# Tails of the output projections by column halves, row sums of the conditioning vector from rounded high and low parts, a work area at a multiple of 64 bytes, and the retention scores at another step

## The reference, cut

```python
mod = silu(c) @ w_ada[i] + b_ada[i]          # 9 x 1024: shift, scale, gate of each sub-layer
h = rms_norm(x, norm_pre[i, j]) * (1 + scale) + shift
y = swiglu_ffn(h, w_in, w_out)               # j = 0, 2: 1024 -> 2 x 2816 -> 1024
y = hybrid_mixer(h, ...)                     # j = 1: retention, pooling, SSD, forgetting attention, gated, @ w_out
x = x + (0.5 or 1) * gate * rms_norm(y, norm_post[i, j])
```

## Time and profile before

| | us |
|---|---|
| median of three executions | 1562.97 |
| lowest, highest | 1561.45, 1563.51 |
| profiled execution | 1561.29 |
| its span, first to last instruction | 1559.5 |
| TensorE busy | 1529.1 |
| mean granted clock | 0.997 |

### The profile page before, as it was taken

One profiled execution on the slowest core, in us unless ns is written; L12 is line 12 of the kernel. 1 busy time (PEld: TensorE's weight loads), 2 busy tenths in 40 slices (PEclk: granted clock), 3 DMA queues, 4 the chain that ended last, 5 costly groups with the idle time before them and its releaser, 6 DMA issues.

```text
span 1559.5 us, 24322 instructions
## 1 busy us (share of the span) xinstructions
PE 1529.1 (98%) x10060; PEld 1390.0 (89%) x10060; DVE 1109.6 (71%) x1311; ACT 761.6 (49%) x947; POOL 165.3 (11%) x96
## 2 busy tenths in 40 slices
PE   7999999999999999999999999999999999999998
PEld 5999879998988889999899998799989788899986
DVE  5887765867896977677666776577878978665453
ACT  3544454556473446444454443554746544554442
POOL 0000002303311110000000000040324011000000
PEclk9999999999999999999999999999999999999999
DMA  9998965656777856788757877375567777555662
GB/s 342 304 312 273 332 181 172 175 153 184 210 237 228 269 175 206 248 268 270 251 185 249 278 255 263 110 224 163 162 203 231 224 246 243 162 173 179 188 190 95
DMA packets 196978, 343.69 MB, mean 220 GB/s; under 512 B 15730, under 2 KB 107122, under 8 KB 196868
## 3 DMA queue, kind: packets, MB, share of 16 engines
q1 hardware_dynamic: 178724, 276.07, 56.3%
q10 hardware_dynamic: 18144, 66.07, 12.9%
HBM read 341.05 MB, written 1.05 MB: 219 GB/s over the span
## 4 chain that ended last, share of the span: by engine, by line
PE 86%; DVE 9%; issue 2%; ACT 2%; DMA 1%; SPq 0%; POOL 0%; DVEq 0%; ACTq 0%; POOLq 0%
PE ps L686 11%; PE ps L689 11%; PE ps L688 10%; PE ps L703 6%; PE ps L702 6%; PE ps L704 6%; PE ps L1015 6%; PE ps L1017 6%; PE ps L1016 6%; PE ps L1077 4%; PE ps L1079 4%; PE ps L1078 4%; DVE w_lo L1412 3%; DVE ada_acc L1428 2%; PE ps L741 1%
## 5 line engine op out<-in xcount | busy, mean ns | idle before, releaser
L1412 DVE TENSOR_TENSOR w_lo<-w_raw,w_hi 128x1024 fp32r<-128x1024 f32 x480 | 614.0, 1298 | 165.2 <-ACT w_hi L1137 164.7
L1137 ACT ACTIVATE w_hi<-w_raw 128x1024 fp32r<-128x1024 f32 x490 | 506.4, 1052 | 345.1 <-DMA w_raw<-in_w_ffn_out 113.8
L686 PE MATMUL ps<-h_hi,w_hi 128*128 128x256 f32 x1408 | 400.3, 285 | 3.5 <-DVE w_lo L1412 2.8
L689 PE MATMUL ps<-h_hi,w_lo 128*128 128x256 f32 x1408 | 398.0, 284 | 0.0
L688 PE MATMUL ps<-h_lo,w_hi 128*128 128x256 f32 x1376 | 390.1, 283 | 0.0
L686 PEld LDWEIGHTS ps<-h_hi,w_hi 128*128 128x128 f32 x1408 | 271.0, 192 | 5.8 <-DVE w_lo L1412 4.0
L689 PEld LDWEIGHTS ps<-h_hi,w_lo 128*128 128x128 f32 x1408 | 271.0, 192 | 0.0
L688 PEld LDWEIGHTS ps<-h_lo,w_hi 128*128 128x128 f32 x1376 | 264.8, 192 | 1.0 <-issue 1.0
L1077 PE MATMUL ps<-h_hi,w_hi 128*128 128x256 f32 x704 | 201.6, 286 | 0.0
L1079 PE MATMUL ps<-h_hi,w_lo 128*128 128x256 f32 x704 | 199.2, 283 | 0.0
L1078 PE MATMUL ps<-h_lo,w_hi 128*128 128x256 f32 x704 | 199.2, 283 | 0.0
(11 more groups left out here) (280 smaller groups left out, 1871.8 us busy)
## 6 DMA issues: line engine op xcount, KB each, us to landing
w_raw<-in_w_ffn_in SPq DMA_DIRECT2D x176, 512.0 KB, 4.6
w_raw<-in_w_in SPq DMA_DIRECT2D x168, 512.0 KB, 3.7
ada_slab<-in_w_ada ACTq DMA_DIRECT2D x126, 512.0 KB, 4.6
w_raw<-in_w_ffn_out SPq DMA_DIRECT2D x88, 512.0 KB, 3.8
ada_slab_first<-in_w_ada SPq DMA_DIRECT2D x16, 512.0 KB, 9.7
w_raw<-in_w_ssm_out SPq DMA_DIRECT2D x16, 512.0 KB, 4.1
w_raw<-in_w_out SPq DMA_DIRECT2D x16, 512.0 KB, 3.6
w_raw<-in_w_pool_out SPq DMA_DIRECT2D x8, 512.0 KB, 3.7
```

Of the source, the lines that this page charges most:

```text
L686: mm(out, wh[:, cs], HH[:, k, :], start=(k == 0 and t == 0), stop=False)
L689: ins = mm(out, wl[:, cs], HH[:, k, :], start=False, stop=(c != 0 and k == KD - 1 and t == 1))
L1137: fn(WH[:, n % N_HI, 0:width], RAW[:, n % N_RAW, 0:width], ACT.Copy).then_inc(w_hi, 1)
L1412: dve.tensor_tensor(WL[:, n % N_RAW, 0:width], RAW[:, n % N_RAW, 0:width], WH[:, n % N_HI, 0:width], ALU.subtract).then_inc(w_lo, 1)
```

## The change

Four things are changed.

- **Column halves in the tail.** Of the six tail chunks the last three (LAST) are now run one column half after the other, so that y is finished in four steps and not in two (`y_ps`). Squares and gates go by halves with them; VectorE now gates the first half, sums the squares, gates the second half and then refines the root. The squares go to SBUF (`squares`, over `gate_silu`), not to PSUM. On the way into a mixer, `shifts` and `h_turn` for tt = 0 stand ahead of the last nine products of the tail; `shifts` and `h_turn` for tt = 1 stand behind the second and third of the four first chunks, and the gate sums behind the fourth. ScalarE and VectorE have the splits of h for tt = 0 ahead of the second half of y there; into a feed-forward sub-layer ScalarE has `x_square` for tt = 1 ahead of `h_hi` for tt = 0.
- **Row sums from two parts.** ScalarE rounds an accumulated row (`ada_acc_hi`), VectorE makes the rest (`ada_acc_lo`, over `ada_acc`), and TensorE sums both in fp32r: four products of fp32r for two of fp32. This adds 11 instructions of 128x1024 to ScalarE and 11 to VectorE, at steps 17/18, 31/32 and 58/59 of feed-forward sub-layers and 95/96 and 102/103 of mixers.
- **Places in SBUF.** The new `one_rounded` moves what stands behind it by 32 bytes: `rstd_diagonal`, `decay_rows` and `row_selector` now begin at an odd multiple of 32 bytes. The work area is rounded to a multiple of 64; it began at 155264 and now begins at 155328.
- **Mixer core.** Step 66 waits only until `newton` has read PSUM (`sstat_read`, its first instruction). The retention scores stand at step 72, where they stood at 71.

```diff
-        work = cursor[0]
+        work = (cursor[0] + 63) // 64 * 64
...
-                    for k in range(n - TAIL, n):
+                    for k in range(n - TAIL, n - LAST):
                         if tt == 0:
                             before(k)
                         wh, wl = weights(BASE[s] + c0 + k)
-                        ins = rows_out(wh, wl, hi, lo, k, tt, False, k == n - 1)
+                        for half in range(2):
+                            ins = half_out(wh, wl, hi, lo, k, tt, half, False, False)
                         if tt:
                             ins.then_inc(w_used, 1)
-                    if tt == 0:
-                        ins.then_inc(y0_ps.sem, 1)
+                    for half in range(2):
+                        if tt and half and s + 1 < SUBS and (s + 1) % 3 == 1:
+                            shifts(s + 1, 0)
+                            h_turn(s + 1, 0)
+                        for k in range(n - LAST, n):
...
+                            ins = half_out(wh, wl, hi, lo, k, tt, half, False, k == n - 1)
+                            if tt and half:
+                                ins.then_inc(w_used, 1)
+                        if not (tt and half):
+                            ins.then_inc(y_ps.sem, 1)
...
+            def column_sums(n, t, bank):
+                pe.wait_ge(acc_hi[n].sem, acc_hi[n].at(t, 1))
+                pe.wait_ge(acc_lo[n].sem, acc_lo[n].at(t, 1))
+                rounded = ONER[:, 0:1].to_broadcast([P, P])
                 for half in range(2):
                     cs = slice(half * HALF, (half + 1) * HALF)
-                    ins = mm(PS[:, bank + half, :], ones, part(1)[:, cs], start=True, stop=True)
-                ins.then_inc(a_ps.sem, 1)
+                    mm(PS[:, bank + half, :], rounded, ACCH[n][:, cs], start=True, stop=False)
+                    ins = mm(PS[:, bank + half, :], rounded, ACCL[:, n * D + half * HALF:n * D + (half + 1) * HALF],
+                             start=False, stop=True)
+                return ins
...
                 if c == 66:
-                    pe.wait_ge(srstd_ok.sem, srstd_ok.at(layer, 1))
+                    pe.wait_ge(sstat_read.sem, sstat_read.at(layer, 1))
...
-                if c == 71:
+                if c == 72:
                     pe.wait_ge(rot_ok.sem, rot_ok.at(layer, 2))
                     pe.wait_ge(yfl_ok.sem, yfl_ok.at(layer, 1))
...
-                pe.wait_ge(yg_ok.sem, yg_ok.at(s - 1, 4))
-                pe.wait_ge(xsq_ok.sem, xsq_ok.at(s, 4))
+                pe.wait_ge(yg_ok.sem, yg_ok.at(s - 1, 3))
+                pe.wait_ge(ysq_ok.sem, ysq_ok.at(s - 1, 3))
                 for j in range(4):
-                    if j == 2:
-                        gate_row_sums(s)
-                        shifts(s, 1)
-                        h_turn(s, 1)
                     if j % 2 == 0:
                         pe.wait_ge(hl_ok.sem, hl_ok.at(s, j // 2 + 1))
                     token_chunk(BASE[s] + j, j, 6, HH, HL, KD, (0,), range(2))
+                    if j == 1:
+                        shifts(s, 1)
+                    if j == 2:
+                        h_turn(s, 1)
+                gate_row_sums(s)
+                pe.wait_ge(yg_ok.sem, yg_ok.at(s - 1, 4))
...
+                fn(ACCH[n][:], part(n), ACT.Copy).then_inc(acc_hi[n].sem, 1)
...
+                dve.tensor_tensor(ACCL[:, n * D:(n + 1) * D], part(n), ACCH[n][:], ALU.subtract).then_inc(acc_lo[n].sem, 1)
```

More of the change, by code:

```diff
@@ L37 @@
 TAIL = 6
+LAST = 3
 N_RAW = 8
@@ L354, in build @@
         CB = at("c_b_products", [P, 2, 384], F32, rk_off)
+        ACCH = {n: at(f"ada_acc_hi{n}", [P, D], F32R, scr_off + i * D * 4) for i, n in enumerate((1, 2))}
         PM = at("pool_m", [P, P * HEADS], F32, rq_off)
@@ L695, in ffn_in, with half_out @@
                 ins.then_inc(w_used, 1)
[L697 to L705, removed]
+            def half_out(wh, wl, hi, lo, k, tt, half, first, last):
+                out = PS[:, 4 + 2 * tt + half, :]
+                cs = slice(half * HALF, (half + 1) * HALF)
+                mm(out, hi[:, k, tok(tt)], wh[:, cs], start=first, stop=False)
+                mm(out, hi[:, k, tok(tt)], wl[:, cs], start=False, stop=False)
+                return mm(out, lo[:, k, tok(tt)], wh[:, cs], start=False, stop=last)
             def out_chunks(s, c0, n, hi, lo, before):
@@ L798, in gate_sums @@
             def gate_sums(t):
-                pe.wait_ge(ada_used.sem, ada_used.at(t, 24))
-                for half in range(2):
-                    cs = slice(half * HALF, (half + 1) * HALF)
-                    ins = mm(PS[:, 4 + half, :], ones, part(2)[:, cs], start=True, stop=True)
-                ins.then_inc(g_ps.sem, 1)
+                column_sums(2, t, 4).then_inc(g_ps.sem, 1)
             def gate_row_sums(b):
                 pe.wait_ge(yg_ok.sem, yg_ok.at(b - 1, 2))
-                pe.wait_ge(xsq_ok.sem, xsq_ok.at(b, 2))
                 gate_sums(b)
@@ L1248, in ffn @@
                         first_h_hi(1)
+                    if s == 0 and c == 17:
+                        acc_hi_part(2, 0)
+                    if s + 1 < SUBS and c == 31:
+                        acc_hi_part(1, s)
+                    if s + 1 < SUBS and c == 58:
+                        acc_hi_part(2, s + 1)
                     split_to(g + 5)
@@ L1371, in mixer @@
                         merged_hi(layer, 0)
+                    if s + 1 < SUBS and c == 95:
+                        act.wait_ge(yrl_ok.sem, yrl_ok.at(layer, 1))
+                        acc_hi_part(1, s)
+                    if s + 1 < SUBS and c == 102:
+                        acc_hi_part(2, s + 1)
                     split_to(g + 5)
@@ L1385, in _ @@
             act.wait_ge(one_ok, 1)
+            fn(ONER[:], one, ACT.Copy)
             x_square(0, 0)
@@ L1642, in merged_lo, with newton @@
                                   ALU.subtract).then_inc(ml_ok.sem, 1)
-            def newton(src, v, r, t, scale, eps):
-                chain(dve.tensor_scalar(v, src, scale, eps, ALU.mult, ALU.add))
+            def newton(src, v, r, t, scale, eps, layer, read=None):
+                ins = dve.tensor_scalar(v, src, scale, eps, ALU.mult, ALU.add)
+                if read is None:
+                    chain(ins)
+                else:
+                    ins.then_inc(read.sem, 1)
+                    dve.wait_ge(read.sem, read.at(layer, 1))
                 chain(dve.tensor_scalar(r.bitcast(I32), v.bitcast(I32), -0.5, float(0x5f3759df), ALU.mult, ALU.add))
```

166 lines of the change are left out of this document (99 added, 67 removed).

## The result

| | before | changed |
|---|---|---|
| median, us (4 executions each) | 1562.59 | 1553.78 |
| lowest, highest | 1561.45, 1563.51 | 1553.27, 1554.53 |
| profiled execution, its span | 1561.29, 1559.5 | 1553.27, 1551.5 |
| TensorE busy | 1529.1 | 1530.8 |

What follows compares the result with a forecast made beforehand. The prediction took TensorE (busy 1529.1 of 1559.5 us) as the bound. Row sums 4.9, mixer boundaries 7.0, feed-forward boundaries 2.9, core 4.8, end 0.4 and places zero gave 20.0 us less: 1543.0 us, range 1538 to 1551.

Runs made afterwards that it cites:

- a_w256: Changed kernel with the work area at 155520, 256 bytes above where it was before the change, weights in place: 1542.12 us, ratio 0.9882.
- a_one_h64: a_one with h_hi and h_lo moved up by 64 bytes and all behind them by 128: 1522.35 us, ratio 0.9753.
- a_one_w192: a_one with h_hi and h_lo in place and all behind them moved up by 192 bytes: 1530.16 us, ratio 0.9792.
- b_w64: Kernel before the change with only the work area moved up by 64 bytes, to 155328: 1572.73 us, ratio 1.0077.
- a_one: Changed kernel with all large tensors back at their old places (dummy inside eps's 32 bytes, work area at 155264): 1542.68 us, ratio 0.9885.

## What to carry to other kernels

A tensor of 4 bytes (32 with its padding) and a start rounded up are a change to every product that reads what was shifted. So freeze the addresses when an edit is to be judged by itself, or print them and compare distances between operands. A cost with a count in the thousands needs a range in nanoseconds, however weak its mechanism looks: 6 ns on 1700 products undid more than half of four careful edits, and 5 ns on 6300 products were lying there to be taken by 128 bytes of padding, though only 20 of their 31 us arrived.

## What the runs showed of the hardware that was not expected

- The rate of rounded products changes with the distance between the stationary and the moving operand in SBUF (stationary minus moving, modulo 256 bytes). For 512 columns: 226.8 to 227.4 ns at 0, 226.8 at 256, 229.6 at 192, and 232.4 to 234.2 at 64, 96, 128, 160 and 224. For 256 columns none is the worst: 119.9 ns at 0, 118.1 to 118.9 at 32, 96 and 128, 117.0 at 192, 115.0 at 64. That 256 is the period is shown by one run (a_w256) and for 512 columns only.
- Moving both operands of the output projections by the same 128 bytes changes nothing (226.8 ns in a_one_h64), nor by the same 192 (226.8 in a_one_w192). A multiple of 64 or 128 as such is of no use: with the work area at 155392, a multiple of 256, it is 232.4 ns.
- The distances are not spread but come in a few values. In the changed kernel the output projections' are almost all 230 to 231 or 235 to 236 ns, before 226 or 227. What sets which product gets which is open, and so is whether the loading of the stationary operand and the stream of the moving one meet in SBUF; no run shows it, and the loads' own rows have the same 188 ns at either pace.
- The Trainium skill ("TensorE: Matmul & The Clock Gate", section "Step-by-step: what each phase is for") gives TensorE two independent read ports into SBUF, one for the moving and one for the stationary operand. Read so that the two reads never slow each other, the distance between the operands should not matter; b_w64, which changes nothing else and is 11.5 us slower, says that it does. Whether the ports have to do with it is open.
- The kernels in which h and the weights stand apart spread more between executions: the four of each lie within 5.1 to 9.9 us, those of a_one within 1.8. The profiled execution of a_one_h64 has two stretches at a granted clock of 0.5, one behind the wait of 4.43 us, that a_one's does not have.
